# RWKV-7 pairs in a software pipeline: the front of a pair over two steps, and W of the lower levels by block transposes

## What is computed

```python
def step(S, inp):
    r_t, w_t, k_t, v_t, kk_t, a_t = inp
    sa = -jnp.einsum('dbhvk,dbhk->dbhv', S, kk_t)
    S = (S * w_t[..., None, :] + sa[..., :, None] * (kk_t * a_t)[..., None, :]
         + v_t[..., :, None] * k_t[..., None, :])
    return S, jnp.einsum('dbhvk,dbhk->dbhv', S, r_t)
```

## Time and profile before

| | us |
|---|---|
| three runs, median | 2802.12 |
| lowest, highest | 2801.75, 2805.22 |
| profiled execution, its time | 2806.61 |
| its span | 2804.8 |
| PE, DVE, ACT busy in the span | 2638.8, 1978.6, 1149.2 |
| mean granted clock of PE | 0.979 |

### The profile page before, as it was taken

How to read it: one execution, slowest core, us unless ns; L and a number is a source line. 1 busy time by engine, 2 the same in 40 slices (tenths; PEclk the granted TensorE clock), 3 DMA queues, 4 the chain that set the end, 5 groups by cost and what they waited for, 6 DMA issues and landing times. The chain is left out here.

```text
span 2804.8 us, 42833 instructions
## 1 busy us (share of the span) xinstructions
PE 2638.8 (94%) x18094; PEld 2197.3 (78%) x18094; DVE 1978.6 (71%) x1855; ACT 1149.2 (41%) x1319; POOL 283.8 (10%) x199
## 2 busy tenths in 40 slices
PE   1999979998899999999999899999999999999996
PEld 1888869997777888888888677888778888888885
DVE  6778956776566878888888778865668755555557
ACT  1443335555434333333333345546443333333332
POOL 0000000000004000000000086541040000000000
PEclk9999989999999999999999899999999999999998
DMA  9999912220546888888888467744568755555552
GB/s 352 330 337 368 372 65 72 72 68 32 210 152 240 328 298 329 302 327 303 325 307 323 134 211 251 271 155 140 189 222 316 270 185 191 194 186 188 194 189 81
DMA packets 252890, 636.73 MB, mean 227 GB/s; under 512 B 10222, under 2 KB 17060, under 8 KB 230596
## 3 DMA queue, kind: packets, MB, share of 16 engines
q1 hardware_dynamic: 246578, 621.84, 62.2%
q10 hardware_dynamic: 6162, 12.72, 1.2%
HBM read 632.42 MB, written 2.10 MB: 226 GB/s over the span
## 5 line engine op out<-in xcount | busy, mean ns | idle before, releaser
L479 DVE TENSOR_TENSOR s_wl<-s_raw,s_wh 128x2048 fp32r<-128x2048 f32 x393 | 913.7, 2325 | 509.4 <-ACT s_wh L474 501.1
L474 ACT ACTIVATE s_wh<-s_raw 128x2048 fp32r<-128x2048 f32 x396 | 758.3, 1915 | 1163.6 <-PE pa L639 503.0
L637 PE MATMUL pa<-s_wh,s_hth 128*128 128x512 f32 x1616 | 646.0, 400 | 17.2 <-DVE s_wl L479 11.4
L639 PE MATMUL pa<-s_wh,s_htl 128*128 128x512 f32 x1616 | 635.0, 393 | 0.0
L638 PE MATMUL pa<-s_wl,s_hth 128*128 128x512 f32 x1616 | 634.6, 393 | 0.0
L637 PEld LDWEIGHTS pa<-s_wh,s_hth 128*128 128x128 f32 x1616 | 307.0, 190 | 92.6 <-DVE s_wl L479 16.1
L639 PEld LDWEIGHTS pa<-s_wh,s_htl 128*128 128x128 f32 x1616 | 306.6, 190 | 65.5
L526 DVE SCALAR_TENSOR_TENSOR s_wide<-s_adaw,s_silu_c,s_wide 128x2048 f32<-128x2048 f32 x150 | 351.8, 2346 | 6.4 <-DMA s_adaw<-in_ada_w 6.4
L638 PEld LDWEIGHTS pa<-s_wl,s_hth 128*128 128x128 f32 x1616 | 307.1, 190 | 60.2
L637 PE MATMUL pb<-s_wh,s_hth 128*128 128x512 f32 (+1 forms) x816 | 318.9, 391 | 0.7 <-DVE s_wl L479 0.7
L639 PE MATMUL pb<-s_wh,s_htl 128*128 128x512 f32 (+1 forms) x816 | 318.6, 390 | 0.0
(11 more groups left out here) (372 smaller groups left out, 2698.2 us busy)
## 6 DMA issues: line engine op xcount, KB each, us to landing
s_raw<-in_ffn_w_in SPq DMA_DIRECT2D x176, 1024.0 KB, 5.2
s_adaw<-in_ada_w SPq DMA_DIRECT2D x160, 1024.0 KB, 6.0
s_raw<-in_ffn_w_out SPq DMA_DIRECT2D x88, 1024.0 KB, 7.5
s_raw<-in_ab_w_in SPq DMA_DIRECT2D x48, 1024.0 KB, 9.0
s_raw<-in_diff_w_in SPq DMA_DIRECT2D x48, 1024.0 KB, 5.2
s_raw<-in_ada_w SPq DMA_DIRECT2D x16, 1024.0 KB, 8.5
s_raw<-in_ab_w_out SPq DMA_DIRECT2D x16, 1024.0 KB, 5.4
s_qkv<-in_ada_w SPq DMA_DIRECT2D x16, 1024.0 KB, 7.2
```

The source lines that it names most:

```text
L474: act.activation(wh[:, s % 2, :, 0:width], raw[:, s, :, 0:width], ACT.Copy).then_inc(hi_done, 1)
L479: dve.tensor_tensor(wl[:, s % 2, :, 0:width], raw[:, s, :, 0:width], wh[:, s % 2, :, 0:width].bitcast(F32), ALU.subtract).then_inc(lo_done, 1)
L637: pe.matmul(o, a_hi, w_hi, start=start and k == 0, stop=False)
L639: mm = pe.matmul(o, a_lo, w_hi, start=False, stop=stop and k == UK - 1)
```

## The change

- The loop begins at t = -3. The front of a pair is spread over two steps: pair m = t+2 ("ahead") gets shifts, mix, sums, clamp, keys, unit_keys, rates, square, norm_ln, norm_exp, exps and bonus; pair n = t+1 ("front") gets factors early in the step, then scores 0 (ahead of level_v(4)), scores 1 (ahead of level_q(5)), its masks, first and level 0. z_turn, z_copy, z_own and decays are for pair q = t+3.
- head_sums stands behind chain_s(1) instead of ahead of level_v(2). outputs(c) stands ahead of the last W instead of behind it.
- level_w for levels 1 to 4 goes, and so does the seed of L3 in first. In their place DVE makes R_W by dve.transpose of R_V, 128x512 in blocks of 32x32 (level_t), after ACT's copy. Up to level 4 the blocks of a unit are 32x32, so this is the whole transpose. The first W stays in R_C0.
- For level 5 ACT copies R_W into L3 (last_seed), and PE adds Q W there (last_w). On ACT's queue level_v(n, 0) and norm_exp(m) stand behind last_seed, exps(m) behind last_w.
- On DVE, the first cond_step of a step stands behind first(n) and ahead of level_t(4), level_q(5) and unit_keys(m).
- Buffers: R_v 3, R_bonus 4, R_g 5, R_dec 4; R_sq goes, its square is in R_rn. Waits follow.

The diff, cut to what orders the work:

```diff
-            def level_w(t, lv):
-
-                act.wait_ge(w_done, 5 * t + lv)
-                act.activation(flat(R_WF if lv == LEVELS - 1 else R_W), L3, ACT.Copy).then_inc(wc_ready, 1)
+            def last_seed(t):
+
+                act.wait_ge(wt_ready, 4 * t + 4)
+                act.activation(L3, flat(R_W), ACT.Copy).then_inc(ws_ready, 1)
+
+            def last_w(t):
+
+                act.wait_ge(w_done, t + 1)
+                act.activation(flat(R_WF), L3, ACT.Copy).then_inc(wf_ready, 1)
...
+                if ahead:
+                    square(m)
                 if chain:
                     chain_x(c, 2)
+                if lev and not gla:
+                    turned_ab(t, 0)
                 if lev:
                     level_v(t, 3)
                 if t == PAIRS:
                     gla_kdt(0)
                 if chain:
                     chain_u(c, 2)
-                if front:
-                    norm_exp(n)
-                if lev:
-                    level_w(t, 3)
-                if t == PAIRS - 1:
+                if ahead:
+                    norm_ln(m)
+                if gla:
                     gla_exp(0)
                     gla_exp(1)
-                if front:
-                    exps(n)
                 if chain:
                     chain_x(c, 3)
-                if lev and t < PAIRS - 1:
-                    turned_ab(t, 0)
+                if lev and not gla:
+                    turned_ab(t, 1)
                 if lev:
                     level_v(t, 4)
-                if t == PAIRS - 1:
+                if gla:
                     act.drain()
                     gla_ln(0)
                 if chain:
                     chain_u(c, 3)
-                if lev and t < PAIRS - 1:
+                if lev and not gla:
+                    turned_v(t)
+                if lev:
+                    last_seed(t)
+                if gla:
+                    turned_ab(t, 0)
+                    turned_v(t)
                     turned_ab(t, 1)
+                if front:
+                    level_v(n, 0)
+                if ahead:
+                    norm_exp(m)
                 if lev:
-                    level_w(t, 4)
-                if t == PAIRS - 1:
-                    turned_ab(t, 0)
-                if lev:
-                    turned_v(t)
-                if t == PAIRS - 1:
-                    turned_ab(t, 1)
-                if lev:
-                    level_w(t, 5)
-                if t == PAIRS - 1:
+                    last_w(t)
+                if gla:
                     gla_ln(1)
                     gla_qk(0)
                     gla_qk(1)
                 if t == PAIRS:
                     gla_exps(2)
+                if ahead:
+                    exps(m)
                 if chain:
                     output(c)
                 if t == PAIRS:
                     gla_exps(3)
-                if m < PAIRS:
-                    z_copy(m)
-                if front:
-                    level_v(n, 0)
-                if m < PAIRS:
-                    z_own(m)
-                    decays(m)
+                if q < PAIRS:
+                    z_copy(q)
+                    z_own(q)
+                    decays(q)
...
-                if n:
-                    dve.wait_ge(w_done, 5 * n)
-                dve.tensor_tensor(R_W[:], R_C0[:], eye2.unsqueeze(1).to_broadcast((P, NU, CH)), ALU.add).then_inc(first_ready, 1)
+                dve.tensor_tensor(R_C0[:], R_C0[:], eye2.unsqueeze(1).to_broadcast((P, NU, CH)), ALU.add).then_inc(first_ready, 1)
 
             def level_q(t, lv):
 
@@ -1940,9 +1938,14 @@
                 dve.tensor_tensor(R_Q[:].rearrange("p (d c) n -> p d c n", d=2), by_chunk(L1), level_mask(lv),
                                   ALU.mult).then_inc(qc_ready, 1)
 
+            def level_t(t, lv):
+
+                dve.wait_ge(vc_ready, 5 * t + lv + 1)
+                dve.transpose(flat(R_W), flat(R_V)).then_inc(wt_ready, 1)
...
+            for t in range(-3, PAIRS + 1):
+                c, n, m, p = t - 1, t + 1, t + 2, t - 2
+                lev, chain, front, ahead = 0 <= t < PAIRS, 0 <= c < PAIRS, 0 <= n < PAIRS, 0 <= m < PAIRS
                 gla = t == PAIRS - 1
-                if t > PAIRS:
-                    break
                 if lev:
                     level_q(t, 1)
                 if gla:
                     normed(p)
                     logits(0)
                 if front:
-                    shifts(n)
-                    mix(n)
+                    factors(n)
+                if ahead:
+                    shifts(m)
                 if chain:
                     state(c, 0)
-                if tail and not gla:
+                if lev:
+                    level_t(t, 1)
+                    level_q(t, 2)
+                if ahead:
+                    mix(m)
+                if 0 <= p and not gla:
                     normed(p)
-                if lev:
-                    level_q(t, 2)
                 if gla:
                     logits(1)
                     logits(2)
                     logits(3)
                     state(c, 1)
-                if front:
-                    sums(n)
-                    clamp(n)
-                if tail:
-                    finish(p)
+                if ahead:
+                    sums(m)
                 if lev and not gla:
                     masked(t, 2)
+                if t >= PAIRS - 1:
+                    finish(p)
                 if t == PAIRS:
                     prods(0)
                 if chain and not gla:
                     state(c, 1)
                 if lev:
+                    level_t(t, 2)
                     level_q(t, 3)
                 if gla:
                     cond_step(dve, 32 + 2 * t)
                     masked(t, 2)
+                if ahead:
+                    clamp(m)
+                    keys(m)
                 if lev:
                     masked(t, 3)
-                if front:
-                    keys(n)
+                if 0 <= p < PAIRS - 3:
+                    finish(p)
                 if chain:
                     state(c, 2)
                 if lev:
+                    level_t(t, 3)
                     level_q(t, 4)
                 if gla:
                     cond_step(dve, 33 + 2 * t)
-                if front:
-                    unit_keys(n)
-                    factors(n)
-                if lev:
-                    level_q(t, 5)
                 if front:
                     masked(n, 0)
                     masked(n, 1)
                     first(n)
                 if lev and not gla:
                     cond_step(dve, 32 + 2 * t)
+                if lev:
+                    level_t(t, 4)
+                    level_q(t, 5)
                 if gla:
                     logs(0)
                     logs(1)
-                if front:
-                    bonus(n)
+                if ahead:
+                    unit_keys(m)
+                    bonus(m)
                 if t == PAIRS:
...
-                    mm = two(unit(L2, u), R_W[:, u], eye2, start=(u == 0))
+                    mm = two(unit(L2, u), R_C0[:, u], eye2, start=(u == 0))
                 mm.then_inc(v_done, 1)
-                if n:
-                    pe.wait_ge(wc_ready, 5 * n)
-                for u in range(NU):
-                    two(unit(L3, u), eye2, R_W[:, u], start=(u == 0))
 
             def level_q(t, lv):
 
@@ -2486,16 +2492,16 @@
 
                 pe.wait_ge(qc_ready, 5 * t + lv)
                 if lv > 1:
-                    pe.wait_ge(wc_ready, 5 * t + lv - 1)
+                    pe.wait_ge(wt_ready, 4 * t + lv - 1)
+                w = R_C0 if lv == 1 else R_W
                 for u in range(NU):
-                    mm = two(unit(L2, u), R_W[:, u], R_Q[:, u])
+                    mm = two(unit(L2, u), w[:, u], R_Q[:, u])
                 mm.then_inc(v_done, 1)
 
-            def level_w(t, lv):
-
-                pe.wait_ge(qc_ready, 5 * t + lv)
-                if lv > 1:
-                    pe.wait_ge(wc_ready, 5 * t + lv - 1)
+            def last_w(t):
+
+                pe.wait_ge(qc_ready, 5 * t + 5)
+                pe.wait_ge(ws_ready, t + 1)
                 for u in range(NU):
                     mm = two(unit(L3, u), R_Q[:, u], R_W[:, u])
                 mm.then_inc(w_done, 1)
...
+            for t in range(-3, PAIRS + 1):
+                c, n, m, q = t - 1, t + 1, t + 2, t + 3
+                lev, chain, front, ahead = 0 <= t < PAIRS, 0 <= c < PAIRS, 0 <= n < PAIRS, 0 <= m < PAIRS
                 gla = t == PAIRS - 1
-                c, n, m = t - 1, t + 1, t + 2
-                lev, chain, front = 0 <= t < PAIRS, 0 <= c < PAIRS, 0 <= n < PAIRS
                 if lev:
                     level_q(t, 1)
                 if chain:
@@ -2675,16 +2683,14 @@
                     gla_low()
                 if t == PAIRS:
                     gla_turn(2)
-                if front:
```

(40 more changed lines are left out.)

116 lines of the change are left out of this document (55 added, 61 removed).

## The result

The changed kernel takes 2848.66 us (median of four runs, 2845.41 to 2851.65), the kernel before beside it 2801.93: the ratio is 1.0162, 95% interval 1.0150 to 1.0174. That is 46.7 us slower where 27 were forecast. The profiled execution of after is the fastest of its four (2845.41 us, span 2843.4), so against the profiled span of before (2804.8) 38.6 us can be traced.

A forecast was written before the change was run, and what follows sets the result against it. PE's instruction stream was taken to bound the loop. Prologue +14.3, steps 0 to 5 +11.6, last steps -3.7 and clock +5 gave +27.2 on 2806.61, 2833.8 us profiled, 2829 as median; range 2806 to 2848.

The forecast's parts named there:

- Rival (a): In the loop, PE's freed time returns: steps of 28.8 us if all waits hid, 2784 us in all; chance 0.12.
- The transposes: On DVE, four 128x512 f32 transposes per pair, taken as 0.65 us each, 1.4 at the dear end.
- First half of a step: level_v(1) to level_v(4): 17.3 us becomes 18.3, level_w leaving, waits for U and Q2 and scores(n,0) coming.
- Second half: level_v(4) to next level_v(1): long path through DVE and ACT makes a step 35.4 us instead of 33.5.
- rival (b): In the loop, only the norm isn't late: steps about 33.0 us, +8 in all, 2810 us; chance 0.10.
- Clock: PE's new stops of 1.6 and 2.6 us lower the granted clock: 1 us in each of five steps, +5.
- Rival (c): Clock falls at both stops of every step: 3 us show in each of six, +40, 2842 us; chance 0.12.
- The signs: What would show the forecast in the trace, among them level_v(1) records 35.4 to 36.5 us apart.
- Step 6: Step from level_v(1) at 609.83, with no ahead part, so no norm_exp or bonus: 30.8 us against 32.2.
- The prologue: Ahead of pair 0, one more loop turn puts its level_v(1) at 429 instead of 414.7 us: +14.3.
- Step 0: First step after pair 0's level_v(1), with no chain: 30.1 us against 28.1, +2.0.
- The step with the gates: Late step with the GLA gates: DVE's logits bind its middle, level_w ahead and behind give back 2.3 us.

The follow-up runs named there:

- the fourth experiment: Block transposes alone put on the kernel before, level_w 1 to 4 and the L3 seed gone, front in one step as before: ratio 0.9994.
- the seventh: Kernel before with block transposes, plus PE reordered so scores 2, scores 3 and turn_ab(1) precede chain_s(0), (1), (2), up_decays after first: ratio 0.9937, 2786.04 us.
- second experiment: Changed kernel with two groups of 16 unused extra products on PE ahead of bonus(m): ratio 1.0137 to the kernel before, step 35.6 us.
- the third experiment: Changed kernel with head_sums of step t = 8 alone put back ahead of level_v(2) and chain_u(1): ratio 1.0141 to the kernel before.
- the fifth: Changed kernel with the front over two steps, but W by level_w products on PE and no transposes: ratio 1.0140 to the kernel before.

## Why the prediction was right and wrong

**What bounds the kernel.** Right that the kernel before is bound by PE's stream, and that PE's freed time doesn't return in this order. Rival (a) falls, and by the fourth experiment it falls already for the transposes alone, before any front is moved; by the seventh it comes true for them once the stops have other cover. A slip in reading: from level_v(1) of pair 0 to that of pair 6 (414.72 to 609.83) are six steps, not 5.8; the sum counts six, so nothing hangs on it.

**The transposes.** 0.65 was assumed; 24 of them in the six steps take 704 ns on average, 0.63 from one start to the next operation (522.46 to 523.09). The estimate of 1.2 us, from the figure of VectorE: DVE Perf Modes of the Trainium skill (The three transpose paths), was too dear. Another page of the Trainium skill (Vector Engine (DVE) Microarchitecture Reference, The reshape front-end and per-opcode configuration) says that the transposing array sustains an element per cycle and lane; the row agrees in so far as a masked pass of the same shape takes 690 ns, while the cycle itself no run here shows.

**First half of a step.** 18.3 to level_v(4) was forecast, 18.57 measured (534.15 to 552.72). The waits at chain_s are 0.72, 0.63 and 0.63 in the brackets. Counted as the sum counted them, from the start of one group to that of the next, chain_s comes 0.89, 0.80 and 0.80 us later than chain_u alone would let it (0.23 us), 2.5 in all against 2.4. The prediction names 0.75 for each, which gives 2.25; its 2.4 was the better number. The wait for Q2 is 0.32, forecast 0.5.

**Second half.** In the step from 534.15, last_seed begins at 26.0 (forecast 25.75), Exp is done at 28.85 (28.62), bonus begins at 30.32 (30.04). PE's stops are 1.41 and 2.42 (1.6 and 2.6). Without the clock the step is 35.6 (second experiment) against 35.4. This was right link by link, and two experiments that cut the chain shorten it. What the cut is worth was wrong in rival (b): it had steps of 33.0 with the norm no longer late, and both experiments gave 34.4 to 34.5, since DVE's own sequence of level_t(4), unit keys, bonus, moments and conditioning steps takes nearly as long.

**Clock.** The mechanism was right. Its size per step was too small and its count too large: 1.3 us in each of t = 2 to 4 and nothing in t = 1 and 5, instead of 1 in each of five. Steps 1 to 5 together were forecast at +14.6 with it and came to +14.3; that two errors cancel to 0.3 us is luck. Rival (c), 3 us in six steps, falls, though its 2842 is nearer to the result than my 2829. The signs gave 35.4 to 36.5 for a step; three of them lie above it, at 36.8 to 36.95.

**The direction, the range and what the sum missed.** Slower was right, at 0.80, and the chain of the second half and the extra turn made it so. The size was not: +27 forecast, +46.7 measured, at the far end of the range. That end was built on transposes of 1.4 us and 3 us of clock in six steps, and neither came; other terms filled the distance, so it is luck that the range reaches this far. The miss against the profiled execution (2845.4 against 2833.8) is in the terms outside the loop's middle, where the count of one step was carried over:
- Step 6: -1.4 forecast, +1.5 measured. I took out norm_exp and bonus and looked for nothing behind them. outputs' copy on ACT, s_R_y, stands behind last_w there, and moments and the conditioning step on DVE behind it, as DVE's and PE's timelines below show. About 1.0 us of the step is the clock, behind a stop of 3.31 us ahead of its level_v(1) (granted 0.57 from 643.5 to 647.5; level_v(2) comes after 6.4 us, 5.4 in the steps before). In the third experiment's trace the same step takes 35.1 us, and 7.9 to level_v(2).

```profile
672.50 0.61 DVE L1966 BATCH_NORM_STATS2 s_R_st<-s_R_y 128x6 f32<-128x64 f32 x4 [2.29 <-ACT s_R_y L1503]
...
677.11 1.19 PE L2369 MATMUL pt<-s_R_Q,s_R_C 64*64 64x64 f32 x30 [3.73 <-DVE s_R_Q L1938]
```

- Step 8: 0 forecast, +4.0 measured. The moved head_sums was costed in a step with levels and not in the one without; the third experiment shows it.
- The prologue: +14.3 forecast, +15.6 measured. Its last part, bonus to level_v(1), was put at "about 6" and took 7.0 (424.03 to 431.00). The third experiment's trace, with the same instructions there, has +13.3 (40.2 us from z_turn to level_v(1), 27.0 in the kernel before), so this miss is within what the clock makes of it from one execution to the next.
- Step 0: +2.0 forecast, +3.0 measured. By filling the stop at bonus it falls from 31.1 to 29.5, which is more than the clock gives back at t = 2 to 4, and I had given it no clock; how the 1.6 us divide is not shown.
- The step with the gates: -2.3 forecast, -0.9 measured. No run took it apart; this stays open.

These are 2.9, 4.0, 1.3, 1.0 and 1.4 us, and 0.6 are there before the stage begins: 11.2, less 0.3 in steps 1 to 5, of the 11.6. The other 8 us of the miss are no mechanism: I subtracted 4.5 because before's profiled execution was above its median, and after's was 3.3 below its own. The two longest runs of after have a mean clock of 0.966 and the profiled one 0.970, which fits to a clock that falls in more steps or for longer. That the steps change from execution to execution the third experiment's trace shows; no trace of such a long run is here.

**What I would not have forecast.** I costed the front at +2.4 for U and +0.5 for Q2 against 2.8 for level_w, so I had seen that the transposes buy nothing in the first half; that they buy nothing in the second either (V's copies, 5.8 us in five steps) I had not. For the fourth experiment I expected 0.9955 to 0.997, and for the fifth 1.008 to 1.010. Both missed because I divided the loss between the two parts; the fourth and fifth experiments put nothing of it on the transposes and 1.4 of the 1.6 per cent on the front.

## What to carry to other kernels

Before removing products from a bound TensorE, write beside each the hand-over that it covers: what it costs is its length less that of the stop it leaves, and here the removal gained 0.3 of 3.6 us. Put other ready work into the stop in the same edit; of the two edits neither gained by itself, and together they took 18 us off. When work moves within one engine's hand-written order, follow it in each special step (first, last, the one with an extra branch) and look at what that engine has queued in front of it, above all an instruction that waits for another engine.

## What the runs showed of the hardware

- A 32x32-block transpose on VectorE of 128x512 f32, SBUF to SBUF, takes 0.70 us, as long as an ordinary pass of that shape.
- Behind stops of 1.41 and 2.42 us (ending at 557.29 and 564.47) the granted clock is 0.57 from 565 to 569, mostly the lower level, in a step where it is 1.00 else; that costs 1.3 us. Behind stops of the same length it stays at 1.00 in other steps, and in which ones differs between two executions of the same instructions (t = 1 and 5 whole in one, t = 2 and 5 undisturbed in the other). Behind stops of 1.41 and 0.55 it is 1.00 at t = 0 to 4.
- An ACT_TABLE_LOAD took 1.28 us and nothing beside it: the copy before it ends at 561.27, the Exp behind it starts at 562.58.
- TensorE's order has a small price of its own. In the kernel of the order alone up_decays (96x128 tiles) stands between groups of 64x64 tiles, where in the kernel before it stands behind a group of 128x128 tiles. From its start to the next group's are 1.06 us, and 0.96 in the kernel before (536.97 to 537.93):

```profile
505.99 1.10 PE L2361 MATMUL pa<-s_R_W,s_cst 64*64 64x64 f32 x32
507.02 1.13 PE L2387 MATMUL pa<-s_raw 96*128 96x256 f32 x4
508.08 1.15 PE L2361 MATMUL py<-s_R_V,s_raw 64*64 64x64 f32 x32
```

The group ahead of it takes 1.03 us instead of 0.94, and what follows z_turn starts 0.31 us after its second part instead of 0.22. These three are most of the 0.33 us by which bonus to level_v(1) is longer there; that the change of tile shape is the cause is not shown.
